# Three reorderings in a hybrid decoder step: the conformer's end, the residual's read-back, attention's end

## The reference

```
h = rmsnorm(x) @ w_in                      # split into the inputs of three mixers
ya = silu(layernorm(causal_conv31(v * sigmoid(g))))      # conformer, 512 wide
yb = s5(u) ;  yc = mamba2(z, silu(causal_conv4(xbc)), dt)
x = x + concat(ya, yb, yc) @ w_out
q = rmsnorm(x) @ wq
x = x + softmax(q k^T / sqrt(512)) v @ wo  # 4 heads, 256 memory tokens
x = x + (silu(causal_conv3(rmsnorm(x) @ w_gate)) * (rmsnorm(x) @ w_up)) @ w_down
```

## Time and profile before

| | us |
|---|---|
| median of 3 runs (1953.63, 1960.84, 1962.93) | 1960.84 |
| the profiled execution | 1955.62 |
| its span, first to last instruction | 1953.6 |
| PE busy in the span | 1893.7 |
| ACT busy | 703.8 |
| DVE busy | 1088.5 |
| mean granted clock of TensorE | 0.979 of full |

### The profile page before, as it was taken

The page is one execution under the profiler, slowest core; times in us unless marked ns, Lnnn a source line. Parts: engine busy times, 40 slices in busy tenths (PEclk is TensorE's granted clock), DMA queues, the critical chain, the costliest instruction groups (busy, mean ns, idle before and its releaser), DMA issues.

```text
span 1953.6 us, 32075 instructions
## 1 busy us (share of the span) xinstructions
PE 1893.7 (97%) x12311; PEld 1690.9 (87%) x12311; DVE 1088.5 (56%) x1923; ACT 703.8 (36%) x1051; POOL 235.2 (12%) x257
## 2 busy tenths in 40 slices
PE   7999999799999999999999999999999999999998
PEld 4866677677777799996599999999999999999997
DVE  4796697564444546444334655555555554555554
ACT  2100152533333334324223444444444434444444
POOL 1023200001122233000013100000000000002300
PEclk9999999999999899999999999999999999999999
DMA  6333363355455646646745455555555555554553
GB/s 203 98 97 91 93 199 110 99 161 163 153 169 172 210 154 218 223 159 259 294 136 163 149 164 167 165 161 163 166 165 161 163 157 162 160 163 156 160 166 105
DMA packets 157953, 316.43 MB, mean 162 GB/s; under 512 B 16938, under 2 KB 39482, under 8 KB 152931
## 3 DMA queue, kind: packets, MB, share of 16 engines
q1 hardware_dynamic: 136146, 296.01, 48.6%
q10 hardware_dynamic: 21723, 19.27, 3.1%
HBM read 300.78 MB, written 14.89 MB: 162 GB/s over the span
## 4 chain that ended last, share of the span: by engine, by line
PE 86%; DVE 3%; ACT 2%; DMA 1%; issue 0%; ACTq 0%; SPq 0%; DVEq 0%
PE bank L698 23%; PE bank L1119 19%; PE bank L1121 19%; PE bank L1120 19%; PE bank L1219 2%; PE bank L1231 1%; PE bank L767 1%; PE bank L752 1%; DVE wlo L2459 1%; PE bank L1241 1%; DVE raw_lo L2286 1%; DMA raw<-in_w_out 1%; PE bank L1062 0%; DMA kv<-in_cache_mem_v 0%; DVE hlo L2481 0%
## 5 line engine op out<-in xcount | busy, mean ns | idle before, releaser
L1119 PE MATMUL bank<-hhi,whi 128*128 128x288 f32 x2128 | 635.4, 299 | 13.0 <-DVE wlo L2459 9.8
L1120 PE MATMUL bank<-hlo,whi 128*128 128x288 f32 x2128 | 632.0, 297 | 0.0
L1121 PE MATMUL bank<-hhi,wlo 128*128 128x288 f32 x2128 | 629.8, 296 | 0.0
L2459 DVE TENSOR_TENSOR wlo<-raw,whi 128x1024 fp32r<-128x1024 f32 (+1 forms) x270 | 330.3, 1224 | 390.0 <-ACT whi L1612 389.7
L1612 ACT ACTIVATE whi<-raw 128x1024 fp32r<-128x1024 f32 (+1 forms) x270 | 283.2, 1049 | 520.8 <-PE bank L1121 509.2
L1119 PEld LDWEIGHTS bank<-hhi,whi 128*128 128x128 f32 x2128 | 402.1, 189 | 14.9 <-DVE wlo L2459 14.6
L1121 PEld LDWEIGHTS bank<-hhi,wlo 128*128 128x128 f32 x2128 | 404.6, 190 | 0.0
L1120 PEld LDWEIGHTS bank<-hlo,whi 128*128 128x128 f32 x2128 | 402.9, 189 | 0.1
L698 PE MATMUL bank<-hT,raw 128*128 128x288 f32 x1024 | 264.7, 418 | 1.2 <-DVE hT L1946 1.2
L698 PEld LDWEIGHTS bank<-hT,raw 128*128 128x128 f32 x1024 | 196.9, 195 | 60.4 <-issue 7.4
L1119 PE MATMUL bank<-ahi,whi 128*128 128x288 f32 x688 | 204.3, 297 | 3.5 <-DVE alo L2696 1.6
(11 more groups left out here) (474 smaller groups left out, 1978.9 us busy)
## 6 DMA issues: line engine op xcount, KB each, us to landing
raw<-in_ffn_w_down SPq DMA_DIRECT2D x86, 512.0 KB, 3.7
raw<-in_ffn_w_gate SPq DMA_DIRECT2D x80, 512.0 KB, 3.6
raw<-in_ffn_w_up SPq DMA_DIRECT2D x80, 512.0 KB, 3.6
raw<-in_w_in SPq DMA_DIRECT2D x64, 512.0 KB, 3.6
raw<-in_xa_wk SPq DMA_DIRECT2D x32, 512.0 KB, 3.8
raw<-in_xa_wv SPq DMA_DIRECT2D x32, 512.0 KB, 4.4
raw<-in_w_out SPq DMA_DIRECT2D x32, 512.0 KB, 3.8
raw<-in_xa_wq SPq DMA_DIRECT2D x32, 512.0 KB, 3.8
```

What stands on the lines that cost most here:

```text
L1119: pe.matmul(out, lhsT=wh[:, wo:wo + P], rhs=xh, start=first, stop=False)
L1120: pe.matmul(out, lhsT=wh[:, wo:wo + P], rhs=xl, start=False, stop=False)
L1121: return pe.matmul(out, lhsT=wl[:, wo:wo + P], rhs=xh, start=False, stop=last)
L2459: tt(wlo[:, s % 2, wsl], raw[:, s % 4, wsl], whi[:, s % 2, wsl].bitcast(F32), ALU.subtract)\
```

## The change

Three places are reordered; no product and no transfer is added or taken out.

1. The first conformer sum moves from slab 61 to slab 58, the second from 63 to 61. DVE centres after eight of the twelve tap tiles. conf_end goes: root, all twelve Silu of xc, Silu of the conformer and its high halves stand in ACT's queue ahead of the memory's first high half, and reciprocal, scaling and low halves in DVE's ahead of the first low half. The first state loads stay at y = 3.
2. ACT issues the read-back of the residual behind the split of G_OUT's slab 5 instead of ahead of slab 2's.
3. SP issues slabs 0 and 1 of G_O ahead of the last cache's wait. ACT and DVE split both before the sample sum is copied. PE makes half of the last piece's values, turns the sample sum, and makes the other half; the sample halves now come before the last piece's halves on both engines, and G_O's first product waits for both.

```diff
@@ -61,7 +61,7 @@
     "dve_norms": (("hmix", 16), ("hxa", 16), ("hffn", 16), ("hfin", 8)),
-    "pe_mixers": (("glu_mm", 4), ("ex_mm", 5), ("conf_mm", 2), ("mem_t", 8), ("ps_t", 1),
+    "pe_mixers": (("glu_mm", 4), ("ex_mm", 5), ("mem_t", 8), ("ps_t", 1),
                   ("os_t", 1)),
...
@@ -349,7 +349,7 @@
-        GLU_AT, EXPORT_AT, CONF_AT = 50, 56, 61
+        GLU_AT, EXPORT_AT, CONF_AT = 50, 56, 58
...
@@ -472,6 +472,8 @@
                         between(s)
+                    if isinstance(g, int) and g == G_O and s < 2:
+                        continue
                     if isinstance(g, int) and g == 0 and s < 4:
...
@@ -511,14 +513,20 @@
                 load_cache(3, t)
+            def wo_slabs(slabs):
+                for s in slabs:
+                    sp.dma_start(slab_dst(s, GW), slab_src(I["xa_wo"][0], s, 0, GW))\
+                      .then_inc(S(f"raw_loaded{s}"), 16)
             for c in range(4, 2 * NB):
+                if c == 2 * NB - 1:
+                    sp.wait_ge(*at("pv_sample", 4))
+                    wo_slabs((0, 1))
                 if c < 12:
...
                     load_cache(c, t)
-            sp.wait_ge(*at("pv_sample", 4))
             four_groups(I["xa_wo"][0], G_O)
...
@@ -892,7 +900,7 @@
                     conf_sum("conv_a", va, 6)
-                if x == CONF_AT + 2:
+                if x == CONF_AT + 3:
                     conf_sum("conf_sq", th, 7)
...
@@ -1191,18 +1199,19 @@
-            def p_values(n):
+            def p_values(n, part=range(4)):
...
                     pe.wait_ge(*at("o_lo", n))
-                for d in range(4):
+                for d in part:
                     for t in range(MT):
...
                                t == 0, t == MT - 1)
-                q.then_inc(S("pv"), 1)
+                if 3 in part:
+                    q.then_inc(S("pv"), 1)
...
@@ -1277,14 +1286,16 @@
                     sample_values(b)
-            p_values(7)
+            p_values(7, (0, 1))
             pe.wait_ge(*at("osum", 1))
...
             x.then_inc(S("os_t"), 1)
+            p_values(7, (2, 3))
...
                 pe.wait_ge(*at("os_lo", 1))
+                pe.wait_ge(*at("o_lo", 8))
             def ff_columns(s):
...
@@ -1551,6 +1562,17 @@
                 a(th[:, t, :], va[:, t, :], ACT.Square).then_inc(S("conf_sq"), 1)
+            sc_.wait_ge(*at("conf_read", 1))
+            a(rstd[:, :], rstd[:, :], ACT.Sqrt).then_inc(S("conf_s"), 1)
+            for t in range(12):
+                sc_.wait_ge(*at("conv_c_taps", t + 1))
+                a(xc[:, t, :], xc[:, t, :], ACT.Silu).then_inc(S("conv_c"), 1)
+            for t in range(4):
+                sc_.wait_ge(*at("conf_scaled", t + 1))
+                a(va[:, t, :], va[:, t, :], ACT.Silu, bias=col(C_LNB + t)).then_inc(S("conf_silu"), 1)
+            for t in range(4):
+                sc_.wait_ge(*at("conf_silu", t + 1))
+                a(hhi[:, t, :], va[:, t, :], ACT.Copy).then_inc(S("cat_a_hi"), 1)
...
@@ -1584,23 +1606,6 @@
                     sc_.dma_start(s0[:, j, :, :], s0_src[j]).then_inc(S(f"s0_loaded{j}"), 16)
-
-            def conf_end(y):
-
-                if y == 0:
-                    a(rstd[:, :], rstd[:, :], ACT.Sqrt).then_inc(S("conf_s"), 1)
-                if y == 1:
-                    for t in range(4):
-                        sc_.wait_ge(*at("conf_scaled", t + 1))
-                        a(va[:, t, :], va[:, t, :], ACT.Silu, bias=col(C_LNB + t)).then_inc(S("conf_silu"), 1)
-                    for t in range(4):
-                        sc_.wait_ge(*at("conf_silu", t + 1))
-                        a(hhi[:, t, :], va[:, t, :], ACT.Copy).then_inc(S("cat_a_hi"), 1)
-                if y in (2, 3):
-                    for t in range(6 * (y - 2), 6 * (y - 1)):
-                        a(xc[:, t, :], xc[:, t, :], ACT.Silu).then_inc(S("conv_c"), 1)
-                if y == 3:
-                    first_s0()
...
@@ -1666,7 +1671,8 @@
                     mem_hi(9 + 2 * y)
-                conf_end(y)
+                if y == 3:
+                    first_s0()
                 if y % 8 == 7:
...
@@ -1690,8 +1696,6 @@
             k_split(NKV + 1)
-            sc_.dma_start(xT[:, :, :], x_spill).then_inc(S("x_back"), 16)
-
             def root(n):
...
@@ -1734,8 +1738,11 @@
                 sc_.wait_ge(*at(f"st_ssd{i}", 16 * 4))
-            for s in range(4, 8):
-                split(G_OUT, s)
+            split(G_OUT, 4)
+            split(G_OUT, 5)
+            sc_.dma_start(xT[:, :, :], x_spill).then_inc(S("x_back"), 16)
+            split(G_OUT, 6)
+            split(G_OUT, 7)
             groups_1_to_3(G_OUT, h_hi_early(C_XA, "x_out"))
...
@@ -1796,15 +1803,17 @@
                         a(dst, src, ACT.Copy).then_inc(S("pTm_a"), 1)
-                if n == 8:
-                    sc_.wait_ge(*at("pv_sample", NB))
-                    a(osum[:, :], B[3][:, :], ACT.Copy).then_inc(S("osum"), 1)
-                o_hi(n - 1)
+                if n < 8:
+                    o_hi(n - 1)
             sc_.wait_ge(*at("s_scores", KQ))
             split(G_O, 0)
+            split(G_O, 1)
+            sc_.wait_ge(*at("pv_sample", NB))
+            a(osum[:, :], B[3][:, :], ACT.Copy).then_inc(S("osum"), 1)
             sc_.wait_ge(*at("os_t", 1))
...
               B[5][:, :].rearrange("p (d h t) -> p h d t", d=4, h=XH), ACT.Copy).then_inc(S("os_hi"), 1)
+            o_hi(7)
...
@@ -1814,7 +1823,7 @@
                .then_inc(S("ff_rows"), 16)
-            for s in range(1, 8):
+            for s in range(2, 8):
                 split(G_O, s)
...
@@ -2263,15 +2272,25 @@
-            for t in range(12):
+            for t in range(8):
                 conv_c(t)
...
                 stt(va[:, t, :], B[6][:, 0:T], -1.0 / 512, va[:, t, :], ALU.mult, ALU.add).then_inc(S("centred"), 1)
+            for t in range(8, 12):
+                conv_c(t)
             v.wait_ge(*at("centred", 4))
...
             ts(rstd[:, :], B[7][:, 0:T], 1.0 / 512, EPS, ALU.mult, ALU.add).then_inc(S("conf_read"), 1)
+            v.wait_ge(*at("conf_s", 1))
+            me.link(v.reciprocal(rstd[:, :], rstd[:, :]))
+            for t in range(4):
+                stt(va[:, t, :], va[:, t, :], col(C_LNW + t), rstd[:, :], ALU.mult, ALU.mult)\
+                    .then_inc(S("conf_scaled"), 1)
+            for t in range(4):
+                v.wait_ge(*at("cat_a_hi", t + 1))
+                tt(hlo[:, t, :], va[:, t, :], hhi[:, t, :].bitcast(F32), ALU.subtract).then_inc(S("cat_a"), 1)
...
@@ -2295,21 +2314,6 @@
                 return tokT[0:w, 3 * q + c, h0:h0 + n].unsqueeze(2).to_broadcast([w, n, HP])
-
-            def conf_end(y):
-
-                if y == 1:
-                    v.wait_ge(*at("conf_s", 1))
-                    me.link(v.reciprocal(rstd[:, :], rstd[:, :]))
-                    for t in range(4):
-                        stt(va[:, t, :], va[:, t, :], col(C_LNW + t), rstd[:, :], ALU.mult, ALU.mult)\
-                            .then_inc(S("conf_scaled"), 1)
-                if y == 2:
-                    for t in range(4):
-                        v.wait_ge(*at("cat_a_hi", t + 1))
-                        tt(hlo[:, t, :], va[:, t, :], hhi[:, t, :].bitcast(F32), ALU.subtract)\
-                            .then_inc(S("cat_a"), 1)
-                    v.wait_ge(*at("cat_a", 4))
...
@@ -2591,14 +2594,17 @@
                         v.tensor_copy(dst, src).then_inc(S("pTm_v"), 1)
-                o_lo(n - 1)
+                if n < 8:
+                    o_lo(n - 1)
             split(G_O, 0)
+            split(G_O, 1)
             v.wait_ge(*at("os_hi", 1))
...
                 .then_inc(S("os_lo"), 1)
-            for s in range(1, 7):
+            o_lo(7)
+            for s in range(2, 7):
                 split(G_O, s)
...
             def ffn_columns():
```

## The result

| | before | after |
|---|---|---|
| median, measured side by side, us | 1961.88 (1953.63 to 1963.39, 4 runs) | 1938.68 (1937.77 to 1944.96, 4 runs) |
| ratio of after to before | | 0.9897, 95% interval 0.9862 to 0.9932 |
| the profiled execution, us | 1955.62 | 1939.30 |
| its span, us | 1953.6 | 1937.4 |

What follows compares the result with a forecast made beforehand. TensorE bounds the kernel, busy 1893.7 of 1953.6 us, so only its idle time or halved clock can yield gains. Gains of 8.7 + 4.9 + 4.1 = 17.7 us from the median 1960.84 give 1943 us, range 1934 to 1952.

Steps and rivals of the forecast that it cites:

- Part 1, the chain on ACT: Conformer's end: neither sum waits, first memory piece 1.3 us late, PE's first wait 3.2 us, then no conformer work in ACT's way.
- Part 1, the size: Memory split: slab 4 starts 9.7 us earlier, less 1.0 for the half clock; gain 8.7 us, ends 4 and 10.
- Part 2: Output weights: the later residual read-back removes a 2.98 us wait and 1.89 us of slow slab; gain 4.87 us.
- The rival's other half: Output weights: slabs behind the residual come late, a 3 us stall plus 1.9 slow; time 1948; residual rival's chance 0.13.
- Part 3: Attention's end: wait before G_O 1.6 us instead of 3.15, no slow slab, no 0.78 us wait; gain 4.1 us.
- The wait did not move forward: Rival, memory split: ACT limits the start and slabs 1 to 4 wait in turn; part 1 gains 4, time 1948; chance 0.12.
- The cache was late: Rival, attention's end: last value cache late behind 1 MB of weights, up to 2.7 us; time 1946; chance 0.06.
- The slower case: Output weights: residual lands far later than 10.9 us and holds later low halves; 1964 at 31 us; chance 0.02.
- The price of a wait: On PE: a wait of about 3 us costs 1.9 us more in the slab behind it, at most 1.88 us nothing.

Runs made afterwards that it cites:

- The hoist without the early sums: Changed kernel with the two conformer sums back at slabs 61 and 63 and centring behind all twelve tap tiles; 1955.98 us.
- part 1 alone: Kernel before with only the conformer's sums and end moved; 1953.24 us against 1966.45, ratio 0.9944.
- part 2 alone: Kernel before with only the residual's read-back moved behind slab 5's split; 1958.22 us, ratio 0.9973.
- the changed kernel again: The changed kernel unedited, run a second time beside two further versions; 1938.57 us, ratio to before 0.9878.
- piece 7's values first: Changed kernel with prompt piece 7's values ahead of the last sample batch and its halves early; 1940.27 us, ratio to before 0.9897.
- residual later: Changed kernel with the residual's read-back behind output-weight slab 7's split instead of slab 5's; no whole time given, a loss of 8.3 us in the trace.
- slabs later: Changed kernel with G_O's two early weight slabs asked for behind the last value cache instead of ahead of it; one execution, 1947.21 us.
- sums without the hoist: Kernel before with the two conformer sums and centring early, conf_end staying among memory slabs 0 to 3; one time, 1973.67 us.
- both edits: Changed kernel with memory slabs 0 and 1 rounded early and piece 7's values ahead of the last sample batch; 1939.11 us, ratio to before 0.9867.

## Why the prediction was right

The forecast was a gain of 17.7 us; the stretches A, C and D give 18.1 (10.58 + 4.72 + 2.84), and the ratio of the times 20.2 (1.03% of 1961.88; 13 to 27 by its interval). From the profiled execution's own time the forecast was 1937.9 against 1939.30. The sum is nearer than its terms, and that is luck: part 1 gave more than was forecast and part 3 less. Means over all traces with the old or the new order at a place say so too: A 31.6 against 21.3, C 27.8 against 22.6, D 17.2 against 15.1, gains of 10.3, 5.1 and 2.1 us. Step by step:

- **Part 1, the chain on ACT: right.** Neither sum waits; the first memory piece starts 0.6 us later (forecast 1.3), PE's first wait is 2.97 us (forecast 3.2) with the half clock behind it, and slabs 1 to 4 start without a wait. The hoist without the early sums shows that the second sum's release sets when the chain starts.
- **Part 1, the size: too small.** The forecast was 8.7 us and A gained 10.6. From slab 0 to slab 1 the forecast has 5.4 us (365.5 to 369.9, and 1.0 for the half clock); the trace has 4.63, as slab 1 waits for nothing and the half clock cost 1.41 (4.63 less the 3.22 of slab 2) and not 1.9. Slabs 2 and 3 were priced at 3.48 us, with the 0.60 that the timeline gives as the length of four transposes; but the next product starts 0.35 after their start (369.05 and 369.40). Measured are 3.22 for slab 2 (373.58 to 376.80) and 4.32 for slab 3 with the token rows (forecast 4.98).
- **Stretch B: 2.70 us longer in the one profiled execution, and in no term of the prediction.** It isn't shown to be a price of the change: before's 270.3 is the shortest B of all thirteen traces. The four traces with conf_end among the memory slabs have 276.7 in the mean, the six with after's order 276.8; and the ten runs of part 1 alone put it at 0.56%, 11 us (7 to 15), about what A gives.
- **Part 2: right.** 4.72 us against 4.87. The landing is at 10.2 us (forecast 10.9) and 0.4 us before DVE wants it (the forecast had it land 0.2 us after DVE was free for it, and 0.7 before PE would miss it). That room is small: the experiment that issues the transfer 6.4 us later loses 8.3 us. The rival's other half, slabs behind the residual, fell: three landed in a median of 6.7 us beside it and none was missed. The Trainium skill (DMA: Bandwidth & Descriptors, "Queues, rings and completion order") has a DMA engine take turns between queues by the packet; the prediction read from this that the residual wins whenever both have work. The queues moved 144 packets and 784 in that window, which is not one for one, so that reading isn't borne out, and no run here shows how the turns go.
- **Part 3: the mechanism right, the size too large.** 2.84 us against 4.1. The wait before G_O was 1.50 us (forecast 1.6), slab 0 ran at the full clock, and the 0.78 before slab 1 is gone: 1.65 + 1.69 + 0.78 = 4.12 us are won there, as forecast. "Behind the cache, in turn, two slabs are asked for instead of four, so I take nothing" is the step that failed: the slabs ahead of the cache cost it 1.2 us here (1.4 in the mean over kernels), which the prediction allowed for only in the lower end of its range. D also differs between executions: 16.17 to 17.65 us in the four traces with the old order, 14.39 to 16.35 in the six with the new one.
- **The rivals.** The wait did not move forward to slabs 1 to 4. The cache was late, by 1.2 us of the 2.7 allowed. The slower case needed a landing 27 us from issue; the longest in any trace was 13.0, in a kernel with the read-back in its old place, and 10.5 in the new one.
- **The price of a wait.** It was read from single waits of one execution. For the waits of the sum it held in kind, but it is no rule: the kernel with part 2 alone ran memory slab 0 slowly behind the same 1.88 us (last section).

## What to carry to other kernels

A chain of small work that one engine's queue mixes into a pipeline can cost more than its length, since later slabs wait behind each piece (8.8 us of ACT's work moved, 10.6 gained in A); it may be worth moving whole, and then what releases its first instruction has to move as well, or next to nothing is won (1.5 us). A read-back has a window: too early and it takes bandwidth from what is needed next, too late and a whole queue stands behind its wait; read both edges from the trace before moving it. Where order alone changes, compare the stretches between events that both kernels have; the sum of these told 18 us here, where single executions differ by up to 13 in a stretch that nobody touched. One trace of each is still one draw: D's gain is 2.8 in this pair and 2.1 in the means.

## What the runs showed of the hardware that was not expected

**The stretch B takes 270.3 to 283.8 us, and the clock makes the difference.** In the five further traces that have the same instructions there as after and an A within 0.2 us of its (the changed kernel again, piece 7's values first, residual later, slabs later, and part 1 alone) it is 273.7, 278.2, 277.4, 280.5 and 278.0, against 273.0. The whole stretch in before, after and the sums without the hoist (length, PE busy, and the granted clock in the third column from the end):

```profile
392.24:662.56 270.32, 264.84 (x1207) 198.32 (x1205) 132.00 (x184) 95.73 (x143) 51.80 (x57) 0.94 0.51 160
381.12:654.14 273.02, 265.73 (x1207) 199.50 (x1206) 133.64 (x187) 96.73 (x145) 51.79 (x57) 0.93 0.52 162
392.71:676.46 283.75, 276.23 (x1206) 204.31 (x1205) 132.02 (x184) 95.78 (x143) 52.84 (x57) 0.89 0.49 152
```

The length times the mean granted clock (to three places 0.935, 0.931 and 0.895), less PE's idle time (5.48, 7.29 and 7.52), is 247.3, 246.9 and 246.4 us, and in all thirteen traces it lies between 246 and 248. So what differs is a little of PE's idle time and, for the most part, how long the clock is halved.

One place where it falls: in the memory stage, PE runs sixteen products four columns wide, and the granted clock falls behind them with PE occupied throughout. The windows of after (PE busy first, the clock in the third column from the end):

```profile
430.00:435.00 5.00, 5.00 (x14) 3.08 (x14) 3.86 (x7) 0.00 (x0) 0.00 (x0) 0.77 0.19 73
435.00:440.00 5.00, 5.00 (x25) 4.15 (x24) 1.23 (x1) 1.59 (x2) 0.00 (x0) 0.89 0.42 111
```

The same windows of the kernel with the slabs behind the cache, whose instructions up to here are the same:

```profile
430.00:435.00 5.00, 5.00 (x12) 2.44 (x12) 2.85 (x6) 0.00 (x0) 0.00 (x0) 0.53 0.31 115
435.00:440.00 5.00, 5.00 (x13) 3.84 (x13) 1.10 (x2) 0.00 (x0) 0.00 (x0) 0.50 0.00 0
```

And its timeline at the fall:

```profile
428.91 2.16 PE L704 MATMUL bank<-xc,s0T 128*128 128x4 f32 x16
431.00 3.78 PE L704 MATMUL bank<-bm,xds 32*128 32x512 f32 x4
```

The four products of L704 at 431.00 take 3.78 us at the half clock; in after they still take 1.98. After's products are slow (0.63 us) from 432.89 to 435.87, 3.0 us; here the clock is half from 431.00 to 440.42, 9.4 us. The Trainium skill (TensorE: Matmul & The Clock Gate, "Part 1: The HAM clock gate (the "warmup" mystery)") says that the moment at which the clock changes differs between runs of one kernel; these traces of the same instructions agree. B has eight such runs of narrow products, and in all thirteen traces each of them is followed by the half clock within 5 us; every other fall in B has a wait of PE just before it (1.77 to 2.92 us). That the narrow products make it fall is argued from this alone; no run takes them out.

**The length of a wait alone doesn't decide the clock.** The prediction priced waits of up to 1.88 us at nothing and of about 3 us with a slow slab. At the places of the sum that held (2.97, 4.15 and, in the experiment, 5.63 us: half clock; 1.16 and 1.50 us: full), but at others it went either way. Two waits of 2.85 us ahead of a weight slab in after, at 765.99 and 1085.92, with the clock behind them (third column from the end):

```profile
766.00:771.00 5.00, 5.00 (x26) 5.00 (x27) 1.54 (x1) 0.00 (x0) 2.12 (x2) 0.66 0.73 247
1086.00:1091.00 5.00, 5.00 (x38) 5.00 (x39) 1.89 (x2) 1.06 (x1) 2.05 (x2) 1.00 0.71 202
```

In the kernel with part 2 alone, memory slab 0 ran at a clock of 0.64 behind its wait of 1.88 us, and the token rows at the full clock behind 2.92 us. Behind 2.17, 2.44 and (sums without the hoist) 2.70 us a sample batch took 1.92 us, full clock, and behind 2.03 us the four transposes took 1.11 us, not 0.60. And in the kernel with piece 7's values first, G_O's slab 0 fell to the half clock 0.6 us into its products behind a wait of 1.46 us, the third in a row (2.44, 0.72, 1.46); with both edits, three such waits (2.19, 0.72, 1.46) left it at the full clock.
